# Constant products in three waits of TensorE, four banks more for one chunk, and part of the last norm moved ahead

## The chip, the cores and the metric

The kernel runs as one program on one core of a Trainium2 chip. Its engines are TensorE (PE, with its weight loads as PEld), VectorE (DVE), ScalarE (ACT), GpSimd (POOL) and SyncE (SP), whose queue issues nearly all transfers. The metric is the device time of one execution in microseconds, taken as the median of several executions. Before the change it is 1439.19 us, from three runs between 1438.46 and 1440.05 us.

## The reference

A trunk of two layers over 256 tokens of 1024 features, all in float32. What the change touches is the end of each layer, the first experts of layer 1, and the end of the whole:

```python
for i in range(DEPTH):                                   # DEPTH = 2
    u = rms_norm(h, attn_norm_g[i]) @ w_in[i]            # then three mixers: convolution, SSD, attention
    h = h + concatenate([y_conv, y_ssd, y_mla]) @ w_out[i]
    hn = rms_norm(h, ffn_norm_g[i])
    if i % 2 == 0:
        h = h + swiglu(hn, dense_w_gate[j], dense_w_up[j], dense_w_down[j])
    else:
        h = h + moe_top2(hn, moe_router[j], moe_w_gate[j], moe_w_up[j], moe_w_down[j])   # 8 experts, 2 a token
    gate = sigmoid(rms_norm(h, ple_norm_g[i]) @ ple_w_gate[i])
    h = h + (p[i] @ ple_w_proj[i]) * gate
return rms_norm(h, final_norm_g)
```

`swiglu(h)` is `(silu(h @ wg) * (h @ wu)) @ wd` with 3584 hidden columns, and `rms_norm(x, g)` is `x * rsqrt(mean(x*x) + 1e-6) * g`.

## The kernel before, in words

Every engine has an instruction stream of its own, written out by hand; semaphores tie the streams together, and an engine works through its stream in order. All weights pass through one ring in SBUF, which SP fills in the order in which PE uses it. A transfer into a slot waits until PE has read what was in it.

**Products in parts.** Most products are made exact with three passes: a weight unit `w` that has landed is split by ACT into a high part (`w_hi`, line 1477 or 1483) and by DVE into the rest (`ring_lo`, line 1985 or 1991), and `product` (lines 637 to 639) adds high by high, high by low and low by high. So a unit goes transfer, ACT, DVE, PE. Plain float32 products show two records each, two passes.

**Layer 0, the mixers.** At the end of the mixers PE makes the attention output (bank "pv"), waits until DVE has taken it (`pe.wait_ge(*banks.taken(("pv", L)))`), transposes it (`y_transposed(2, 0)`, line 902), makes the variance product of the convolution (line 911) and the other transposes, and then starts the output projection.

**End of layer 0.** `ple(0)` makes the gates of the embedding add in four groups: half 0 and 1 of the columns, tokens t = 0 and 1. For each group ACT takes the sigmoid (line 1926), DVE multiplies and adds into `h` (lines 2325 and 2329). The norm of layer 1 needs the sum of squares of each group (`square`, line 1501). Before, groups 0 and 1 are squared early and groups 2 and 3 after the last sigmoid and a table load (line 1489); then the roots (1520), the reciprocal (1972), a diagonal matrix of the factors (1977), and PE transposes and scales `h` in one step by 32 passes (line 660). The projections of layer 1 follow.

**The experts.** They are worked in pairs: a heavy one (128 rows, products in parts, `heavy_in`) and a light one (64 rows, plain float32, `light_in`, line 1154) beside each other, in groups of four units of one and four of the other. A unit is 128 x 1792 float32 (0.92 MB); an expert has 48: for each of two chunks of hidden columns 8 units of the gate and 8 of the up matrix, then 16 of the down matrix. The ring has 8 slots for them. The first pair starts with the 16 heavy units of its first chunk, none of the light expert beside them. The gate product of a chunk fills banks 0 to 3; ACT takes the silu out of them (line 1787); then the up product fills the same banks 0 to 3, so its first unit waits for the silu (`g_free`); then DVE multiplies both (line 2481, `gated`), and the gate product of the next chunk waits for that (`u_free`). Banks 4 to 7 belong to the light expert and to transposes.

**The end.** After the last expert, `last_x(0)` transposes half of `h` (line 658), ACT and DVE split it (1529 and 2002), and PE makes the gates of layer 1. After the last add into `h` come the last square, the roots, the reciprocal, and four steps of DVE (line 2674), each `xs = h * rstd * gfin` over 128 x 512; after each one SP writes that quarter out (line 1435). `gfin` is the final norm weight, spread over the partitions.

## Time and profile before

| what | value |
|---|---|
| median of 3 runs | 1439.19 us (1438.46 to 1440.05) |
| the profiled execution, its own time | 1440.5 us |
| its span, first to last instruction | 1438.7 us |
| PE busy | 1387.9 us (96%), mean granted clock 0.991 |
| DVE busy | 854.1 us (59%) |
| ACT busy | 695.3 us (48%) |
| moved by DMA | 443.89 MB, mean 309 GB/s |

The profile is of one execution. Busy shares are means over stages that have different limits: layer 0 runs to about 398 us, the front of layer 1 and the routing to about 538, the experts to about 1400, and the rest is the last embedding add and the last norm. PE's granted clock is a share of full speed: 1.00 is 2.4 GHz and 0.50 is 1.2 GHz.

### The profile page before, as it was taken

The page shows a single profiled execution, that of the slowest core. Times are in us where ns is not written, and L with a number is a line of the kernel's source. Part 1 is how long each engine was busy: PE and PEld are TensorE (multiplying, and loading weights), DVE is VectorE, ACT ScalarE, POOL GpSimd, SP SyncE. Part 2 cuts the span into 40 slices and gives each one's busy share as a digit, 9 for nine tenths or more (in the row PEclk, how much of TensorE's full clock was granted, in tenths as well). Part 3 has the DMA queues.
Part 4 walks back from the last instruction along what each step waited for, and adds up shares of the span by engine and source line. Part 5 has one row for each costly group of instructions (what it writes and reads, how often), then busy time and mean ns, then how long its engine had stood idle before and what let it go on. Part 6 is the DMA issues. An engine that isn't in the chain of part 4 may idle for free.

```text
span 1438.7 us, 18295 instructions
## 1 busy us (share of the span) xinstructions
PE 1387.9 (96%) x6999; PEld 1007.7 (70%) x6999; DVE 854.1 (59%) x986; ACT 695.3 (48%) x783; POOL 6.9 (0%) x14
## 2 busy tenths in 40 slices
PE   6999999999989998999999999999999999999996
PEld 6878888888887787766666666666666666666535
DVE  6997645463479978646454656454656455565425
ACT  6556534542555657544444444444444454544315
POOL 0000000000000000000000000000000000000000
PEclk9999999999999999999999999999999999999998
DMA  9425565555544009999999999999999999999992
GB/s 326 159 69 172 177 199 180 177 200 181 176 136 146 8 8 418 363 421 419 419 405 418 419 419 420 414 404 419 418 420 418 416 412 419 418 419 419 419 410 80
DMA packets 99669, 443.89 MB, mean 309 GB/s; under 512 B 7728, under 2 KB 22096, under 8 KB 99328
## 3 DMA queue, kind: packets, MB, share of 16 engines
q1 hardware_dynamic: 98688, 439.30, 78.1%
q0 software_dynamic: 896, 3.44, 0.7%
q8 instruction: 56, 0.92, 0.3%
q14 instruction: 29, 0.24, 0.0%
HBM read 440.61 MB, written 2.10 MB: 308 GB/s over the span
## 4 chain that ended last, share of the span: by engine, by line
PE 83%; DMA 7%; DVE 6%; ACT 2%; issue 1%; DVEq 0%; ACTq 0%; SPq 0%
PE psum L637 19%; PE psum L638 18%; PE psum L639 18%; PE psum L1154 11%; PE psum L1168 7%; DMA ring<-in_moe_w_up 4%; DMA ring<-in_moe_w_down 3%; PE psum L682 2%; PE psum L1066 1%; PE psum L700 1%; PE psum L660 1%; ACT w_hi L1483 1%; DVE arena_a L2078 1%; PE psum L1183 1%; DVE ring_lo L1991 1%
## 5 line engine op out<-in xcount | busy, mean ns | idle before, releaser
L1991 DVE TENSOR_TENSOR ring_lo<-ring,w_hi 128x1792 fp32r<-128x1792 f32 x191 | 384.3, 2023 | 281.1 <-ACT w_hi L1483 279.0
L1483 ACT ACTIVATE w_hi<-ring 128x1792 fp32r<-128x1792 f32 x191 | 323.3, 1700 | 289.2 <-DMA ring<-in_moe_w_down 121.1
L639 PE MATMUL psum<-w_hi,hidden_b 128*128 128x512 f32 x624 | 230.1, 369 | 0.0
L1985 DVE TENSOR_TENSOR ring_lo<-ring,w_hi 128x2048 fp32r<-128x2048 f32 (+1 forms) x68 | 152.6, 2266 | 102.5 <-ACT w_hi L1477 102.4
L1154 PE MATMUL psum<-ring,xT 128*64 128x512 f32 (+1 forms) x1024 | 201.7, 543 | 0.0
L637 PE MATMUL psum<-w_hi,hidden_b 128*128 128x512 f32 (+1 forms) x512 | 191.3, 374 | 5.2 <-ACT arena_b L1787 3.4
L638 PE MATMUL psum<-ring_lo,hidden_b 128*128 128x512 f32 (+1 forms) x512 | 187.7, 367 | 0.0
L637 PE MATMUL psum<-w_hi,xT_parts 128*128 128x512 f32 (+1 forms) x384 | 150.4, 392 | 4.0 <-DVE xT_parts L2002 3.4
L637 PE MATMUL psum<-w_hi,hidden_a 128*128 128x512 f32 (+1 forms) x384 | 146.7, 382 | 3.6 <-DVE ring_lo L1991 3.6
L1154 PEld LDWEIGHTS psum<-ring,xT 128*64 128x64 f32 x1024 | 69.8, 137 | 114.1 <-issue 112.0
L639 PE MATMUL psum<-w_hi,xT_parts 128*128 128x512 f32 (+1 forms) x384 | 149.2, 389 | 0.0
L638 PE MATMUL psum<-ring_lo,xT_parts 128*128 128x512 f32 (+1 forms) x384 | 149.1, 388 | 0.0
L638 PE MATMUL psum<-ring_lo,hidden_a 128*128 128x512 f32 (+1 forms) x384 | 143.1, 373 | 0.0
L1477 ACT ACTIVATE w_hi<-ring 128x2048 fp32r<-128x2048 f32 (+1 forms) x68 | 126.3, 1898 | 29.2 <-PE psum L639 27.8
L639 PEld LDWEIGHTS psum<-w_hi,hidden_b 128*128 128x128 f32 x624 | 117.6, 188 | 20.8
L637 PEld LDWEIGHTS psum<-w_hi,hidden_b 128*128 128x128 f32 x512 | 96.8, 189 | 34.0 <-issue 9.5
L1168 PE MATMUL psum<-ring,xT 128*64 128x512 f32 (+1 forms) x512 | 112.8, 545 | 0.6 <-DMA ring<-in_moe_w_down 0.6
L638 PEld LDWEIGHTS psum<-ring_lo,hidden_b 128*128 128x128 f32 x512 | 96.9, 189 | 16.0
L639 PE MATMUL psum<-w_hi,hidden_a 128*128 128x512 f32 (+1 forms) x272 | 99.3, 365 | 0.0
L637 PEld LDWEIGHTS psum<-w_hi,hidden_a 128*128 128x128 f32 x384 | 72.3, 188 | 21.3 <-DVE ring_lo L1991 9.3
L637 PEld LDWEIGHTS psum<-w_hi,xT_parts 128*128 128x128 f32 x384 | 72.7, 189 | 18.4 <-DVE ring_lo L1996 3.6
L639 PEld LDWEIGHTS psum<-w_hi,xT_parts 128*128 128x128 f32 x384 | 72.5, 189 | 14.2
(333 smaller groups left out, 1448.3 us busy)
## 6 DMA issues: line engine op xcount, KB each, us to landing
ring<-in_moe_w_gate SPq DMA_DIRECT2D x128, 896.0 KB, 8.9
ring<-in_moe_w_up SPq DMA_DIRECT2D x128, 896.0 KB, 9.9
ring<-in_moe_w_down SPq DMA_DIRECT2D x128, 896.0 KB, 9.8
ring<-in_w_in SPq DMA_DIRECT2D x16, 1024.0 KB, 5.7
ring<-in_dense_w_gate SPq DMA_DIRECT2D x14, 1024.0 KB, 5.1
ring<-in_dense_w_up SPq DMA_DIRECT2D x14, 1024.0 KB, 5.1
ring<-in_dense_w_down SPq DMA_DIRECT2D x14, 1024.0 KB, 4.9
ring<-in_w_out SPq DMA_DIRECT2D x8, 1024.0 KB, 5.0
```

The source lines that it names most:

```text
L637: mm(o, a[0], b[0], start=first, stop=False)
L638: mm(o, a[0], b[1], start=False, stop=False)
L639: return mm(o, a[1], b[0], start=False, stop=final)
L660: last = mm(o[:, c:c + P], h[:, t, kt * P:kt * P + P], diag[:, t, :], start=True, stop=True)
L682: last = mm(o[:, m * SEQ:m * SEQ + SEQ], w[:, kt, m * P:m * P + P], xT[kt], start=kt == 0, stop=kt == KT - 1)
L700: last = mm(o[:, 0:n], xT[kt][:, t * P:t * P + P], w[:, q, :], start=kt == 0, stop=kt == KT - 1)
L1154: last = mm(psum[half * LIGHT:half * LIGHT + LIGHT, 4 + b, 0:n], xl[:, kt, :], w[:, a:a + n], start=kt == 0, stop=kt == KT - 1)
L1168: last = mm(psum[half * LIGHT:half * LIGHT + LIGHT, 2 if tail else 6, c0:c0 + n], elT(kt), w[:, a:a + n], start=kt == 0, stop=kt == FKT - 1)
L1477: A(high(g, sizes[g]), raw(g, sizes[g]), ACT.Copy).then_inc(hi_ready, 1)
L1483: A(heavy_high(c), moe_raw(m), ACT.Copy).then_inc(hi_ready, 1)
L1985: V.tensor_tensor(low(g, sizes[g]), raw(g, sizes[g]), f32(high(g, sizes[g])), ALU.subtract).then_inc(lo_ready, 1)
L1991: V.tensor_tensor(moe_low(m), moe_raw(m), f32(heavy_high(c)), ALU.subtract).then_inc(lo_ready, 1)
```

## The change

A new helper `keep_running(n, b)` makes `n` plain float32 products of constants (the identity by 512 columns of the parameters) into bank `b`, whose content nobody needs. It is called in three places: once with one product ahead of the wait for "pv" in layer 0, once with four after `ple(0)`, once with three after `last_x(0)`.

The first pair's first up chunk goes to banks 4 to 7 (`up_bank`), so that it doesn't wait for the silu, and the next gate chunk waits for the silu instead of for `gated`. The light expert's first gate chunk and the transposes of the heavy hidden part wait for `gated` of that chunk.

In layer 0 the square of group 2 moves ahead of the last sigmoid (it stood there in layer 1 already). In layer 1 DVE multiplies each group of `h` by the final norm weight as soon as it is added (`gained`), and the last step is then one factor a token: DVE does it for t = 0, ACT for t = 1, and SP writes the quarters by halves instead of by tokens.

```diff
+            def keep_running(n, b):
+
+                pe.wait_ge(banks.free[b], banks.count[b])
+                for _ in range(n):
+                    mm(psum[:, b, :], ident, par[:, 0:512], start=True, stop=True)
...
+                if L == 0:
+                    keep_running(1, 3)
                 pe.wait_ge(*banks.taken(("pv", L)))
                 y_transposed(2, 0)
...
                 if L == 0:
                     dense()
                     ple(0)
+                    keep_running(4, 4)
...
             last_x(0)
+            keep_running(3, 3)
...
+        def up_bank(i, ch):
+
+            return 4 if isinstance(i, int) and i == 0 and ch == 0 else 0
...
+                b0 = up_bank(i, ch) if u else 0
+                if b0 and kt == 0:
+                    pe.wait_ge(lx_ready, 1)
                 for b in range(4):
                     if kt == 0 and b < 2:
                         if u:
-                            pe.wait_ge(g_free, half_done(i, ch, b))
+                            if not b0:
+                                pe.wait_ge(g_free, half_done(i, ch, b))
+                        elif ch and up_bank(i, ch - 1):
+                            pe.wait_ge(g_free, half_done(i, ch - 1, b))
                         elif ch:
                             pe.wait_ge(u_free, half_done(i, ch - 1, b))
...
-                    last = product(psum[:, b, 0:cols.stop - cols.start], at((xg_hi, xg_lo), ALLP, kt), at(w, ALLP, cols),
+                    last = product(psum[:, b0 + b, 0:cols.stop - cols.start], at((xg_hi, xg_lo), ALLP, kt), at(w, ALLP, cols),
...
                 elif kt == 0 and ch:
                     pe.wait_ge(lu_free, ch_done(i, ch - 1))
+                elif kt == 0 and up_bank(i, 0):
+                    pe.wait_ge(u_free, half_done(i, 0, 1))
...
-                pe.wait_ge(u_free, half_done(i, ch, (t0 + n - 1) // RUN))
+                pe.wait_ge(u_free, half_done(i, ch, 1 if up_bank(i, ch) else (t0 + n - 1) // RUN))
...
-                    flat = psum[:, 0:4, :].rearrange("p b c -> p (b c)")
+                    flat = psum[:, up_bank(i, ch):up_bank(i, ch) + 4, :].rearrange("p b c -> p (b c)")
...
-            for t in range(NT):
-                for half in range(2):
-                    sp.wait_ge(out_ready, 2 * t + half + 1)
-                    c = slice(half * 512, half * 512 + 512)
+            for half in range(2):
+                c = slice(half * 512, half * 512 + 512)
+                for t, there in enumerate((out_ready, out_scaled)):
+                    sp.wait_ge(there, half + 1)
                     sp.dma_start(out[0, t * P:t * P + P, c], xs[:, t, c]).then_inc(out_done, 16)
...
-                    norm(3 * L, h_added, squared=2)
+                    norm(3 * L, h_added, squared=3)
...
-                        if L == DEPTH - 1 and half and t:
-                            square(3 * DEPTH, 2, h_added)
+                        if half and t:
+                            square(3 * L + 3, 2, h_added)
...
             norm(3 * DEPTH, h_added, squared=3)
+            act.wait_ge(last_rstd, 1)
+            act.wait_ge(gained, 4)
+            for half, buf in enumerate((sg, hs)):
+                A(xs[:, 1, half * 512:half * 512 + 512], buf[:, 1, :], ACT.Copy, scale=rstd[:, 1:2]).then_inc(out_scaled, 1)
...
                         V.tensor_tensor(v, v, buf[:, t, :], ALU.add).then_inc(h_ready, 1)
+                        if L:
+                            if half == t == 0:
+                                dve.wait_ge(gfin_in, 16)
+                            dve.wait_ge(h_ready, 4 * L + 2 * half + t + 1)
+                            V.tensor_tensor(buf[:, t, :], v, gfin[:, cols], ALU.mult).then_inc(gained, 1)
...
             means_of(k, by_half=True)
-            rstd_of(k)
-            dve.wait_ge(gfin_in, 16)
-            for t in range(NT):
-                for c in (slice(0, 512), slice(512, D)):
-                    V.scalar_tensor_tensor(out=xs[:, t, c], in0=h[:, t, c], scalar=rstd[:, t:t + 1], in1=gfin[:, c],
-                                           op0=ALU.mult, op1=ALU.mult).then_inc(out_ready, 1)
+            dve.wait_ge(rms_ready, NT * (k + 1))
+            V.reciprocal(rstd, rms).then_inc(last_rstd, 1)
+            dve.wait_ge(last_rstd, 1)
+            dve.wait_ge(gained, 4)
+            for half, buf in enumerate((sg, hs)):
+                V.tensor_scalar(xs[:, 0, half * 512:half * 512 + 512], buf[:, 0, :], rstd[:, 0:1], None,
+                                ALU.mult).then_inc(out_ready, 1)
```

## Rows read from the trace of the kernel before

**Rows 1.** The page, part 2: GB/s in 40 slices of 36 us.

```profile
GB/s 326 159 69 172 177 199 180 177 200 181 176 136 146 8 8 418 363 421 419 419 405 418 419 419 420 414 404 419 418 420 418 416 412 419 418 419 419 419 410 80
```

**Rows 2.** Waits of PE: who waited for whom, us in total, times, longest.

```profile
PE psum L660 <- DVE xs L1977: 15.8, 2, 11.1
```

**Rows 3.** Windows: busy time by engine, PE's granted clock, DMA share, GB/s.

```profile
402.00:404.00 2.00, 0.97 (x4) 0.98 (x5) 1.68 (x4) 2.00 (x3) 0.00 (x0) 0.50 0.41 140
...
1402.00:1404.00 2.00, 0.00 (x0) 0.00 (x0) 2.00 (x2) 2.00 (x3) 0.00 (x0) 0.50 1.07 414
```

**Rows 4.** Timeline, plain float32 products: start us, us, what, count, idle before.

```profile
99.36 1.12 PE L873 MATMUL psum<-arena_a,par 128*128 128x512 f32 x2
...
537.60 3.81 PE L1056 MATMUL psum<-small,xs 128*128 128x128 f32 x32 [0.86 <-DVE small L2424]
```

**Rows 5.** Timeline of PE and DVE around the "pv" wait of layer 0.

```profile
104.65 0.89 PE L902 MATMUL psum<-par,xs 128*128 128x128 f32 x4 [1.54 <-DVE xs L2249]
...
108.66 0.75 DVE L2001 TENSOR_TENSOR xT_parts<-psum,xT_parts 128x256 fp32r<-128x256 f32 x2
...
109.51 0.47 PE L637 MATMUL psum<-w_hi,xT_parts 128*128 128x512 f32 x1 [0.51 <-issue]
```

**Rows 6.** Timeline of ACT, DVE and PE from layer 0 to layer 1.

```profile
399.76 0.69 DVE L2329 TENSOR_TENSOR h<-h,arena_b 128x512 f32<-128x512 f32 x1
...
400.43 0.61 ACT L1501 ACTIVATE xs<-h 128x512 f32<-128x512 f32 x1
...
403.03 6.54 PE L660 MATMUL psum<-xs,h 128*128 128x128 f32 x32 [4.75 <-DVE xs L1977]
...
409.29 0.19 PEld L637 LDWEIGHTS psum<-xT_parts,w_hi 128*128 128x128 f32 x1
```

**Rows 7.** Timeline of the first pair: PE at both waits, DVE's and ACT's splits.

```profile
569.21 0.77 PE L637 MATMUL psum<-w_hi,hidden_b 128*128 128x512 f32 x1 [3.43 <-ACT arena_b L1787]
...
571.49 3.96 DVE L1991 TENSOR_TENSOR ring_lo<-ring,w_hi 128x1792 fp32r<-128x1792 f32 x2 [2.60 <-ACT w_hi L1483]
...
587.25 1.71 ACT L1483 ACTIVATE w_hi<-ring 128x1792 fp32r<-128x1792 f32 x1 [0.42 <-DMA ring<-in_moe_w_gate]
...
591.66 0.47 PE L637 MATMUL psum<-w_hi,hidden_b 128*128 128x512 f32 x1 [1.27 <-DVE arena_b L2481]
...
608.15 1.70 ACT L1483 ACTIVATE w_hi<-ring 128x1792 fp32r<-128x1792 f32 x1 [1.29 <-DMA ring<-in_moe_w_gate]
```

**Rows 8.** Windows of 10 us after the first chunk, columns as in rows 3.

```profile
580.00:590.00 10.00, 10.00 (x52) 8.47 (x51) 8.11 (x5) 6.96 (x5) 0.00 (x0) 1.00 0.97 379
590.00:600.00 10.00, 8.73 (x47) 7.09 (x46) 4.71 (x4) 0.60 (x1) 0.00 (x0) 1.00 0.96 348
600.00:610.00 10.00, 10.00 (x52) 5.33 (x51) 6.89 (x5) 7.29 (x5) 0.00 (x0) 1.00 0.98 331
```

**Rows 9.** Timeline of PE after the last expert, to its last instruction.

```profile
1404.86 0.77 PE L637 MATMUL psum<-w_hi,xT_parts 128*128 128x512 f32 x1 [3.41 <-DVE xT_parts L2002]
...
1409.54 1.03 PE L658 MATMUL psum<-par,h 128*128 128x128 f32 x8
1410.33 0.48 PE L637 MATMUL psum<-w_hi,xT_parts 128*128 128x512 f32 x1
...
1429.24 0.39 PE L639 MATMUL psum<-w_hi,xT_parts 128*128 128x512 f32 x1
```

**Rows 10.** Timeline of the last norm and of the writes.

```profile
1433.37 2.74 DVE L2674 SCALAR_TENSOR_TENSOR xs<-h,tiny,arena_a 128x512 f32<-128x512 f32 x4
...
1434.15 2.32 SPq L1435 DMA_DIRECT2D out<-xs  x4
```

**Rows 11.** Window at the writes' end, columns as in rows 3.

```profile
1436.00:1438.00 2.00, 0.00 (x0) 0.00 (x0) 0.11 (x1) 0.00 (x0) 0.00 (x0) 0.50 0.90 335
```

**Rows 12.** Two windows that have PE waits, columns as in rows 3.

```profile
850.00:860.00 10.00, 8.21 (x43) 4.73 (x42) 7.73 (x6) 6.80 (x4) 0.00 (x0) 1.00 1.01 419
...
1400.00:1402.00 2.00, 1.19 (x8) 0.76 (x8) 2.00 (x4) 0.94 (x3) 0.00 (x0) 1.00 1.07 392
```

More of the change, by code:

```diff
@@ L366, in trunk @@
             "ptok_in", "last_ptok_in", "gfin_in", "out_ready", "out_done"))
+        out_scaled, last_rstd, gained = sem("out_scaled"), sem("last_rstd"), sem("gained")
         table_in, eps_ready = sem("table_in"), sem("eps_ready")
@@ L2327, in embed @@
                             dve.wait_ge(*banks.taken(("pp", L, half, t)))
-                        v = h[:, t, half * 512:half * 512 + 512]
+                        cols = slice(half * 512, half * 512 + 512)
+                        v = h[:, t, cols]
                         V.tensor_tensor(v, v, buf[:, t, :], ALU.add).then_inc(h_ready, 1)
+                        if L:
[3 more added lines that the diff above has]
+                            V.tensor_tensor(buf[:, t, :], v, gfin[:, cols], ALU.mult).then_inc(gained, 1)
                     if L == 0 and half == 0:
```

## The prediction

> **What bounds the kernel now.** I read the page first. From 540 us to about 1400 us it shows 404 to 421 GB/s in every slice but one, the one from 575 to 611 us, which has 363 [rows 1]. So the experts are bound by their transfers. Only in that slice do the transfers fall short, and time saved on PE among the experts counts only where PE holds back a transfer. All else runs at far lower rates and is bound by PE or by chains between PE, ACT and DVE.
>
> Then the waits of PE. The longest is for the diagonal matrices ahead of the transposes of a layer, 15.8 us in two, of which 11.1 us is the start of the kernel, which nothing here touches; the other is 4.7 us [rows 2]. Then the granted clock in windows: behind that wait PE works at 0.50, and so it does behind the last expert [rows 3]. The timelines show what each wait is for and what is late next.
>
> **Three waits with constant products.** The price of a product: one of 128x512 in plain float32 takes 1.12 us alone, in two passes [rows 4]. That is the upper end for each in a row; for the lower, 32 passes of 128 columns take 3.81 us, 0.12 each [rows 4]. Passes overlap, so I take 0.9 a product, an estimate from below 1.12.
>
> *Layer 0, "pv".* PE idles 1.54 us before 104.65 [rows 5], so one product fits (1.12 at most). What PE does next at the half clock could be faster, but the first product of the output projection starts at 109.51, right after DVE's part of the transposes ends (108.66 + 0.75 = 109.41 [rows 5]), and DVE comes there from the norm factors and a split of weights, not from PE. From there PE has work without a pause. So nothing is gained: 0, with 0 to 1 us for executions in which the clock falls a little later and is still low after 109.51.
>
> *Into layer 1.* Four products behind the last gate (PE idle from 403.03 - 4.75 = 398.28 [rows 6]) end between 398.28 + 4 x 0.9 = 401.9 and 398.28 + 4 x 1.12 = 402.8. The wait now ends at 403.03, and by the next edit at 402.57, so at worst they cost 0.2. Before, PE did nothing from 398.28, its clock was at 0.50 by 402 [rows 3], and the 32 transposing passes took 6.54 us [rows 6]. The same number of passes of the same 128 columns at the full clock took 3.81 [rows 4]. Gain: 6.54 - 3.81 = 2.7. What is late next: ACT and DVE split each of four banks, 0.85 us each on both, beside PE; the first projection needs the banks one after the other, and its first weight load came at 409.29, behind the transposes [rows 6], so I let it follow them.
>
> *The square moved ahead.* ACT's squares start at 400.43 and take 0.61 each [rows 6]; one of the two goes to a place where ACT idles, ahead of the last sigmoid. The remaining one can't start before DVE's add is done, 399.76 + 0.69 = 400.45, later by 0.09 because the sigmoid now waits for the moved square: 400.54 and a handover of 0.04, against a start of 401.04 (400.43 + 0.61). Gain 0.46, let me call it 0.5. Together 3.2 us into layer 1. That part is a chain of PE, then DVE, and its transfers are far from full (146, 8 and 8 GB/s [rows 1]), so I pass all 3.2 on to the start of the experts' loads.
>
> *After the last expert.* PE idles 3.41 us before 1404.86 [rows 9], waiting for DVE; three products end between 1401.45 + 2.7 = 1404.2 and + 3.36 = 1404.8, inside it. Behind it PE works at 0.50: the 12 products up to the transposes at 1409.54 take 4.68 us. At the full clock 84 products run from 1410.33 to 1429.24 [rows 9], 0.228 each, and 12 take 2.73. Gain 1.95. The weights and the second half of the transposed rows then have to come 1.95 earlier; they hang on PE's own transposes, and the splits of the later units have over 1 us to spare, so I take 1.9.
>
> **The first up chunk in banks of its own.** PE stands 3.43 us before 569.21 for the silu and 1.27 us before 591.66 for DVE's product of the chunk [rows 7]; both waits go, and the clock doesn't drop behind the first. PE could go on at 565.8. A unit takes it 9 x 0.228 + 3 x 0.114 = 2.4 us, so the fourth is due at 573.0; its low part comes from DVE, which starts it at 571.49 with 3.96 us for two [rows 7], so it is there at 573.5: 0.5 us lost. Another 0.5 goes to the first transposes of the hidden part, which now wait for all of DVE's product. PE still gains about 5 us. But the loads gain only what they had lost for want of free slots: from 580 to 610 us they moved 379, 348 and 331 GB/s [rows 8] against 420, which is (41 + 72 + 89) x 10 / 420 = 4.8 us. The landings show less: two splits of ACT that waited for their load start at 587.25 and 608.15 [rows 7], eight loads of 0.92 MB apart, 20.9 us where 420 GB/s give 17.5: 3.4 lost. I take the middle, 4.1, and keep 3.4 to 4.8. From 610 us on the loads run full in either kernel, so all later events move by the same 4.1. The lights' new wait and the chunk's wait for the silu are over long before they are reached.
>
> **The last norm.** Before, four steps of DVE take 2.74 us from 1433.37 [rows 10]; after, two short ones on DVE and two of 0.62 on ACT (its square has the same width [rows 6]), so the last quarter is ready about 1.3 us sooner. The added four products with the weight, 0.69 each, lie in DVE's waits for the gates, except the last: it stands before DVE's share of the mean, which ACT's root needs, and costs 0.1. The wait for the weight's transfer moves ahead with them; POOL issues it right behind the last expert, long before DVE reaches the first of the four, and I cost it at nothing. But the writes are 1.05 MB. DVE made a quarter of 262 kB every 0.685 us, 383 GB/s, and in the last window the DMA engines are busy 0.90 of the 2 us [rows 11], though the writes end near 1437.8: they were already saturated. So the end follows the first issue, 1434.15 [rows 10], not the last. The first quarter's step reads one operand from memory where the old one read two; no row has it at this width, it lies between 0 and 0.69, and I take 0.45. The first issue then comes 0.69 - 0.45 - 0.1 sooner. Gain 0.2, from -0.1 to 1.3 if the writes do speed up.
>
> **Sum.** 0 + 3.2 + 4.1 + 1.9 + 0.2 = 9.4 us. The profiled execution took 1440.5 (span 1438.7 and 1.8 around it), which gives 1431.1; the median of the runs is 1.3 lower, 1439.19, and from it I get 1429.8.
>
> **The rivals.**
>
> *The last fall of the clock comes anyway.* Ahead of it, in 1400 to 1402 us, PE was busy for 1.19 of 2.00 us, nearly all of it transposes, and the clock fell at the end. In 850 to 860 us, PE stood still for 1.79 us among ordinary products and the clock stayed at 1.00 [rows 12]. So the transposes may not have held it, and three products behind them may come too late; part of them would then run at half speed and PE would start some 0.7 late, with the clock back sooner than before. From 1.9 to about 0.6: 1431.1. The Trainium skill, page "TensorE: Matmul & The Clock Gate", section "Part 4: PE-mode transpose", says that transposes in that mode don't count as PE work for the clock in the way that products do; by that rule this rival would be the likelier one. The trace agrees as far as those two windows go.
>
> *The loads keep their pace.* If the loss from 580 to 610 us came from the order of loads of heavy and light units and not from PE, the 4.1 are gone: 1433.9. Against it: each load waits for a slot that PE frees, and they are short right after PE's two waits.
>
> *The products don't hold the clock at all.* Then 0.5 is left of the 3.2, and three products at half speed, up to 6.7 - 1.12 = 5.6 us, delay PE by some 2 us from 1404.86 in place of helping; with the clock back at 1408.8 as before this costs 0.8. 0.5 + 4.1 - 0.8 + 0.2 = 4.0: 1435.2.
>
> *Slower.* PE comes to the second pair with more lead than the loads (5 against 4.1), so it waits there for longer. If the clock fell in such waits, as it did in the 3.43 us of the first pair, each fall would cost PE 1.6 us (8 products at 0.43 in place of 0.228), and loads behind it. About eight waits like that of 850 to 860 [rows 12] are spread over the pairs. From the sixth fall on the gain is gone; all eight give 1429.8 + 12.8 = 1442.6. Against it: that wait of 1.79 us left the clock at 1.00, and the lead is used up after one pair.
>
> **How the numbers follow.** My forecast 0.62, the last clock fall 0.16, loads keep their pace 0.09, products don't hold 0.07, slower 0.03, and 0.03 for two of the failures together (about 1438). The range 1427.5 to 1434.3: below the forecast lie 0.7 of the loads (4.8), up to 1 in layer 0 and up to 1.1 in the writes, not all at once; above it the next two rivals. A measurement of this kernel tells about 0.2%, 2.9 us. Faster than 1436.3 are the first four cases nearly always: 0.92. Within 0.2%: 0.05. Slower: 0.03.
>
> **What would show it.** In the new profile: the clock at 1.00 through 400 to 412 us and the transposes in about 3.8 us; no wait of PE for the silu, and over 400 GB/s in each window from 580 to 610 us; the clock at 1.00 behind the last expert, the 12 products in 2.7 us; the writes still at about 380 GB/s from first to last. The prediction is wrong if the experts' part is as long as before, if a later window falls below 400 GB/s by as much as the first pair won, or if PE is late behind its products.

## The result and the profile after

The changed kernel takes 1428.67 us (median of 4 runs, 1428.14 to 1431.9) against 1438.83 before (4 runs, 1438.36 to 1440.05): a ratio of 0.993, 95% interval 0.9916 to 0.9944, so 10.2 us less. The forecast was 1429.8 and the range 1427.5 to 1434.3.

The profiled executions stand further apart, 1428.27 against 1440.5. Four marks that both traces have divide their 12.2 us: the landing of the first of the experts' loads, of the 40th (PE's two waits in the first pair lie before it), of the last, and the end of PE.

```
                                   before    after   less
start to first landing             541.98   537.82   4.16
first to 40th landing               94.11    88.92   5.19
40th to last landing               758.88   757.29   1.59
last landing to PE's end            34.65    33.48   1.17
PE's end to the end                  9.04     8.95   0.09
```

Not all of it is sure to belong to the change. PE is 0.96 us ahead at the output projection of layer 0, and it was so already at 25 us, where nothing was edited. Nothing was edited between the 40th and the last landing either. That stretch takes 757.0 to 757.8 us in nine profiles of kernels with the four banks and 757.5 to 759.4 in five without them, so the two sets overlap and one pair can't tell. Without these two, 4.16 - 0.96 + 5.19 + 1.17 + 0.09 = 9.65 us are left.

The three places of the constant products, in the changed kernel. First the timeline of PE at "pv", against [rows 5] (start us, us, what, count, idle before):

```profile
101.99 1.08 PE L674 MATMUL psum<-par 128*128 128x512 f32 x2
...
103.68 0.66 PE L913 MATMUL psum<-par,xs 128*128 128x128 f32 x4 [0.62 <-DVE xs L2276]
...
108.55 0.47 PE L642 MATMUL psum<-w_hi,xT_parts 128*128 128x512 f32 x1 [1.78 <-DVE ring_lo L2012]
```

One product is two passes, 1.08 us. What follows it is quicker, but the first product of the output projection now waits 1.78 us for DVE and starts 0.96 us sooner than before, the same 0.96 that PE was ahead from 25 us on.

Then DVE, ACT and PE into layer 1, against [rows 6]:

```profile
396.84 0.63 ACT L1524 ACTIVATE xs<-h 128x512 f32<-128x512 f32 x1 [1.48 <-DVE h L2357]
...
397.18 3.59 PE L674 MATMUL psum<-par 128*128 128x512 f32 x8
...
398.89 0.69 DVE L2357 TENSOR_TENSOR h<-h,arena_b 128x512 f32<-128x512 f32 x1
...
399.62 0.63 ACT L1524 ACTIVATE xs<-h 128x512 f32<-128x512 f32 x1
...
401.62 3.84 PE L665 MATMUL psum<-xs,h 128*128 128x128 f32 x32 [0.85 <-DVE xs L2004]
...
405.19 0.19 PEld L642 LDWEIGHTS psum<-xT_parts,w_hi 128*128 128x128 f32 x1
```

The second square stands alone behind DVE's last add, the other is at 396.84, ahead of the sigmoid. The four products take 3.59 us, the transposes 3.84 in place of 6.54, and the first projection starts 4.10 us sooner than before: 3.1 more than the 0.96 that were there already.

Then PE after the last expert, against [rows 9], and the windows there and into layer 1, against [rows 3] (busy time by engine, PE's granted clock, DMA share, GB/s):

```profile
1389.53 1.45 PE L663 MATMUL psum<-par,h 128*128 128x128 f32 x7 [0.27 <-DVE h L2535]
1390.78 4.00 PE L674 MATMUL psum<-par 128*128 128x512 f32 x6
1394.22 0.79 PE L642 MATMUL psum<-w_hi,xT_parts 128*128 128x512 f32 x1
...
1397.39 1.03 PE L663 MATMUL psum<-par,h 128*128 128x128 f32 x8
```

```profile
402.00:404.00 2.00, 2.00 (x21) 2.00 (x20) 2.00 (x2) 1.78 (x4) 0.00 (x0) 1.00 0.00 1
...
1390.00:1392.00 2.00, 2.00 (x7) 1.46 (x6) 2.00 (x3) 1.82 (x5) 0.00 (x0) 0.50 1.07 397
...
1394.00:1396.00 2.00, 2.00 (x8) 1.32 (x7) 2.00 (x3) 0.00 (x0) 0.55 (x1) 1.00 0.67 277
```

Into layer 1 the clock stays at 1.00. After the last expert it falls all the same, during the transposes and before the products, which therefore take 4.00 us; but it is back when the 12 products begin, and they take 3.17 us in place of 4.68.

The first pair, in windows of 10 us against [rows 8]. No window is short of transfers any more:

```profile
570.00:580.00 10.00, 10.00 (x51) 8.45 (x50) 9.11 (x5) 6.97 (x5) 0.00 (x0) 1.00 1.01 424
580.00:590.00 10.00, 10.00 (x55) 8.44 (x54) 8.72 (x7) 4.29 (x4) 0.00 (x0) 1.00 1.01 419
590.00:600.00 10.00, 10.00 (x51) 5.29 (x50) 4.74 (x3) 5.61 (x4) 0.00 (x0) 1.00 1.01 418
600.00:610.00 10.00, 10.00 (x54) 8.07 (x54) 5.17 (x4) 3.50 (x5) 0.00 (x0) 1.00 1.02 421
```

Last, the norm and the writes, against [rows 10]:

```profile
1421.43 1.33 ACT L1969 ACTIVATE xs<-arena_b,tiny 128x512 f32<-128x512 f32 x2 [0.23 <-DVE tiny L2704]
1421.43 0.88 DVE L2708 TENSOR_SCALAR xs<-arena_b,tiny 128x512 f32<-128x512 f32 x2
1421.95 1.82 SPq L1458 DMA_DIRECT2D out<-xs  x4
```

The four writes are issued within 1.82 us in place of 2.32. They land at 1423.99, 1424.70, 1425.37 and 1426.05; before at 1436.22, 1436.90, 1437.58 and 1438.26. Both are 0.67 to 0.71 us apart, and the last lands 4.10 and 4.11 us after the first issue. The 0.5 us that the last issue gained is gone before it lands.

### The profile page after: what moved, and what is told of

It reads as the page before. It is cut to its first block, busy times and chain, and to the rows that moved or that the text cites. A ratio compares the mean times of both kernels' runs of the same rounds, so it can differ in the third digit from the quotient of the medians.

```text
span 1426.5 us, 18333 instructions
## 1 busy us (share of the span) xinstructions
PE 1387.9 (97%) x7015; PEld 1004.9 (70%) x7015; DVE 854.5 (60%) x988; ACT 697.4 (49%) x785; POOL 6.9 (0%) x14
## 4 chain that ended last, share of the span: by engine, by line
PE 84%; DMA 6%; DVE 6%; ACT 2%; issue 1%; ACTq 0%; DVEq 0%; SPq 0%
PE psum L642 19%; PE psum L643 18%; PE psum L644 18%; PE psum L1176 11%; PE psum L1190 7%; DMA ring<-in_moe_w_up 4%; DMA ring<-in_moe_w_down 2%; PE psum L693 2%; PE psum L1080 1%; PE psum L711 1%; ACT w_hi L1506 1%; PE psum L1205 1%; DVE arena_a L2105 1%; DVE ring_lo L2018 1%; PE psum L665 1%
```

## The experiments

The theory to be tested: the loads of the first pair carry half of the gain, and they gain what they were short of, not what PE gains; the clock carries nearly all of the rest, in two places; "pv" and the last norm carry nothing. The first four kernels put one part each into the kernel before.

**The four banks alone.**

```diff
+        def up_bank(i, ch):
+            return 4 if isinstance(i, int) and i == 0 and ch == 0 else 0
...
-                    last = product(psum[:, b, 0:cols.stop - cols.start], ...
+                    last = product(psum[:, b0 + b, 0:cols.stop - cols.start], ...
```

> The kernel before with the four banks for the first pair's first up chunk and nothing else. Theory 'transfers' (the gain is what the loads lost for want of free slots): the slices from 580 to 610 us move over 410 GB/s, the loads of the first pair's end come 4.0 us sooner, and the time falls by 4.0 to 4.8 us although PE gains 5 us or more in that pair. Rival 'PE': all that PE gains is passed on, 5.5 to 6 us. Rival 'the load that came late': of the 5.2 us that the changed kernel gained there, 1.2 us was one load that came late in the one profiled execution of the kernel before; then the medians differ by 4.0 and no more.

Measured: 1433.69 us (6 runs, 1431.84 to 1434.63) against 1439.01 (29 runs, 1435.94 to 1444.11, which the four kernels share): a ratio of 0.9964 (0.9952 to 0.9977), 5.3 us less. The 40th load lands 89.6 us after the first, against 94.1 before. The windows from 580 us:

```profile
580.00:590.00 10.00, 10.00 (x51) 8.46 (x50) 9.28 (x6) 6.80 (x4) 0.00 (x0) 1.00 1.01 422
590.00:600.00 10.00, 10.00 (x55) 7.50 (x56) 4.24 (x5) 3.25 (x4) 0.00 (x0) 1.00 1.03 419
600.00:610.00 10.00, 10.00 (x53) 6.45 (x50) 7.29 (x4) 5.16 (x4) 0.00 (x0) 1.00 1.00 391
```

Two windows are full, the third lacks 29 x 10 / 420 = 0.7 us. So this part is the largest. Its 5.3 lies above the 4.1 of the forecast, but the interval of the ratio, 3.3 to 6.9 us, has room for all three: the theory (4.0 to 4.8), "PE" (5.5 to 6) and "the load that came late" (4.0). The load that came late in the kernel before (the 39th, by 1.2 us) was no accident of one execution: in each of the four other profiles of kernels without the banks, that load or the one before it loses another 0.5 to 0.9.

**The four products into layer 1 alone.**

```diff
                     dense()
                     ple(0)
+                    keep_running(4, 4)
```

> The kernel before with the four constant products into layer 1 and nothing else; the square stays where it was. Theory 'clock': the 32 passes that transpose take 3.8 us in place of 6.5, everything after comes 2.7 us sooner up to the experts' first loads and stays so to the end: 2.7 us less. Rival 'the loads take it back': the experts' loads begin no sooner or wait for something else, and less than 1 us is left at the end.

Measured: 1435.98 us (12 runs, 1434.48 to 1439.93), ratio 0.9984 (0.9975 to 0.9994): 3.0 us less by the medians, 2.3 (0.9 to 3.6) by the ratio. The products and the transposes take as long as in the changed kernel:

```profile
397.55 3.60 PE L669 MATMUL psum<-par 128*128 128x512 f32 x8
...
402.46 3.84 PE L660 MATMUL psum<-xs,h 128*128 128x128 f32 x32 [1.31 <-DVE xs L1984]
```

Its profile shows something else at the first pair. The wait for the silu is the same as in [rows 7], but the clock didn't fall behind it: the first window is this kernel's, the second the kernel before's.

```profile
565.57 0.47 PE L637 MATMUL psum<-w_hi,hidden_b 128*128 128x512 f32 x1 [3.41 <-ACT arena_b L1794]
```

```profile
568.00:572.00 4.00, 4.00 (x22) 3.37 (x21) 4.00 (x3) 3.00 (x2) 0.00 (x0) 1.00 1.02 425
```

```profile
568.00:572.00 4.00, 2.79 (x7) 2.24 (x8) 1.40 (x2) 3.99 (x5) 0.00 (x0) 0.64 1.01 399
```

**The three products after the last expert alone.**

```diff
             last_x(0)
+            keep_running(3, 3)
```

> The kernel before with the three constant products after the last expert and nothing else. Theory 'the clock falls before the products and is back after them' (as in the changed kernel's trace): the products run at half speed, some 4 us for the three, and end about when PE's wait ends; the 12 products behind them run at the full clock, 3.2 us in place of 4.7, and 1.6 us is gained. If the clock falls later in this kernel, by the place of its end, the products themselves or the first of the 12 run slow and 0.6 us is left. Rival 'the products only delay': no gain, or up to 0.8 us lost.

Measured: 1437.04 us (11 runs, 1434.76 to 1439.72), ratio 0.9988 (0.9976 to 0.9999): 2.0 us less by the medians, 1.7 (0.1 to 3.5) by the ratio. PE:

```profile
1398.44 1.75 PE L658 MATMUL psum<-par,h 128*128 128x128 f32 x7 [0.27 <-DVE h L2509]
1399.99 3.53 PE L669 MATMUL psum<-par 128*128 128x512 f32 x6
1402.95 0.79 PE L637 MATMUL psum<-w_hi,xT_parts 128*128 128x512 f32 x1
...
1406.12 1.04 PE L658 MATMUL psum<-par,h 128*128 128x128 f32 x8
```

The clock falls before the products here too and is back at their end; the 12 products take 3.17 us. From the last landing to the first product behind the second transposes it is 14.05 us, against 15.36 before: 1.3 gained in these two executions.

**The last norm alone.**

```diff
-            for t in range(NT):
-                for half in range(2):
-                    sp.wait_ge(out_ready, 2 * t + half + 1)
...
+                for t, there in enumerate((out_ready, out_scaled)):
+                    sp.wait_ge(there, half + 1)
...
+                            V.tensor_tensor(buf[:, t, :], v, gfin[:, cols], ALU.mult).then_inc(gained, 1)
```

> The kernel before with the changed last norm and nothing else (the products with the weight ahead, the second half of the last step on ACT, the writes in the other order). Theory 'writes bind': the first write is issued 0 to 0.2 us sooner and the last lands as long after it as before (4.1 us): 0 to 0.2 us gained. Rival 'the last quarter binds': the last write is issued 0.5 us sooner after the first, so it lands 0.5 us sooner or more: 0.5 to 1.3 us gained.

Measured: 1439.15 us (11 runs, 1435.17 to 1440.54), ratio 1.0003 (0.9994 to 1.0012): nothing. The last write lands 4.10 us after the first issue, and the interval excludes the rival's 1.3 us, though not its 0.5; the landings exclude that.

By the medians the four parts give 5.3 + 3.0 + 2.0 - 0.1 = 10.2 us, the whole 10.2. That they agree to a tenth is luck: by the ratios they are 5.2 + 2.3 + 1.7 - 0.4 = 8.8, each known to some 1.3 to 1.8 us, and the square is in none of them.

**The writes on two queues**, in the changed kernel, to see what binds them.

```diff
-                    sp.dma_start(out[0, t * P:t * P + P, c], xs[:, t, c]).then_inc(out_done, 16)
+                sp.dma_start(out[0, 0:P, c], xs[:, 0, c]).then_inc(out_done, 16)
...
+                act.dma_start(out[0, P:2 * P, c], xs[:, 1, c]).then_inc(out_done, 16)
```

> The changed kernel with the two writes of the second 128 rows issued by ACT, right behind its own scaling, in place of SP. Theory 'the writes bind, at the rate of the memory or the DMA engines': they land 0.68 us apart as before, and the end stays within 0.1 us of 4.1 us after the first issue. Rival 'one queue binds': the two queues' writes land side by side, and the end comes 0.5 us sooner.

Measured: 1429.36 us (5 runs, 1427.94 to 1429.5), ratio 0.9929 (0.9916 to 0.9943). The issues:

```profile
1423.09 0.83 SPq L1457 DMA_DIRECT2D out<-xs  x2
1423.33 0.95 ACTq L1972 DMA_DIRECT2D out<-xs  x2
```

They land at 1425.14, 1425.88, 1426.53 and 1427.18, the last 4.09 us after the first issue, though the last is issued 0.85 us behind the first in place of 1.37. Two queues move no more than one. While the writes are under way the DMA engines are full in both kernels; the first window is the changed kernel's, the second this one's:

```profile
1424.00:1425.00 1.00, 0.00 (x0) 0.00 (x0) 0.00 (x0) 0.00 (x0) 0.00 (x0) 0.50 1.01 375
```

```profile
1424.00:1425.00 1.00, 0.00 (x0) 0.00 (x0) 0.00 (x0) 0.00 (x0) 0.00 (x0) 0.50 1.01 383
```

So the writes bind there (262 kB in 0.68 us, 385 GB/s), and what the last norm gains behind its first issue is lost before the end. The median is 1.2 us above that of the unchanged kernel in the same series (1428.16), so the second queue gained nothing either. Writes of another size were not tried.

**Three products in front of the first up chunk**, in the changed kernel: how much of PE's gain the loads needed.

```diff
                 if b0 and kt == 0:
                     pe.wait_ge(lx_ready, 1)
+                    for _ in range(3):
+                        mm(psum[:, b0, :], ident, par[:, 0:512], start=True, stop=True)
```

> The changed kernel with three constant products put ahead of the first pair's first up chunk, where PE no longer waits: PE is held up there by some 2.8 us at the full clock. Theory 'the loads have a little slack': PE gained about 1 us more in that pair than the loads took, and 0.5 us of it was a wait for DVE's split that the products now cover; so 1.3 to 1.8 us are lost, and they are missing in the slices from 580 to 610 us. Rival 'PE is not what holds the loads': nothing is lost. Rival 'PE holds them at every step': all 2.8 us are lost.

Measured: 1431.68 us (6 runs), ratio 0.9942 (0.9928 to 0.9956). That is 3.0 and 3.5 us above the two medians of the changed kernel (1428.67, and 1428.16 in the run after the next): more than the theory's 1.3 to 1.8, and nearest to the rival "PE holds them at every step" with its 2.8. But the six lie in two groups: 1429.2, 1429.7, 1430.3, and 1433.1, 1433.3, 1433.8. The profile is of the second:

```profile
540.00:550.00 10.00, 10.00 (x44) 8.77 (x44) 8.29 (x7) 7.92 (x7) 0.00 (x0) 0.66 1.02 425
...
590.00:600.00 10.00, 10.00 (x55) 7.27 (x55) 4.39 (x5) 4.60 (x4) 0.00 (x0) 1.00 1.00 370
600.00:610.00 10.00, 10.00 (x53) 6.69 (x50) 6.18 (x4) 4.00 (x3) 0.00 (x0) 1.00 0.98 375
```

Here the clock was low from 541 to 548 us as well, which makes PE later still. The first group lost 0.5 to 2.1 us, which is the theory's size, but these three have no profile, and that no fall came there in them isn't shown. So the theory is neither shown nor out; "nothing is lost" is out by the medians.

**Three products in the wait for the silu**, in the kernel before: what of the gain was the clock.

```diff
+                if u and kt == 0 and ch == 0 and isinstance(i, int) and i == 0:
+                    pe.wait_ge(lx_ready, 1)
+                    for _ in range(3):
+                        mm(psum[:, 4, :], ident, par[:, 0:512], start=True, stop=True)
```

> The kernel before with three constant products in PE's wait for the silu of the first pair (into bank 4): the wait stays, the clock doesn't fall behind it. Theory 'two parts' (the executions in which the clock happened not to fall there missed 3.1 and 3.8 us of loads from 580 to 610 us, those in which it fell 4.8): 1.0 to 1.8 us gained, and the rest needs the wait to go. Rival 'it was the wait alone': 0. Rival 'it was the clock alone': 4 us or more.

Measured: 1438.67 us (11 runs, 1437.46 to 1439.51) against 1439.63 (17 runs), ratio 0.9995 (0.9986 to 1.0004): 1.0 us less by the medians, at most 2.0 by the ratio, and it may be nothing. "The clock alone" is out. The profile can't tell the other two apart: the clock fell at 544 us in it, PE came late to the wait, and the products then held it up. ACT has the first half of the silu at 568.6, PE goes on at 569.67. That is 28.7 us after the first landing, where the last norm alone, whose clock fell in the same place, has 27.6.

```profile
567.69 1.73 ACT L1791 ACTIVATE arena_b<-psum 128x896 f32<-128x896 f32 x2 [0.82 <-PE psum L639]
...
567.50 2.73 PE L1108 MATMUL psum<-par 128*128 128x512 f32 x6
569.67 0.80 PE L637 MATMUL psum<-w_hi,hidden_b 128*128 128x512 f32 x1
```

**The changed kernel once more.**

> The changed kernel unchanged, for the spread of its own executions beside those with single edits: 1428.5 us, with some executions 1.5 to 3.5 us longer. Theory 'falls of the clock at the experts' first products make the long ones': a profile of a short one shows the clock at 1.00 from 530 to 600 us.

Measured: 1428.16 us (5 runs, 1427.91 to 1428.42). No execution was long, and the profiled one of 1427.91 had the low clock from 540 to 547 us:

```profile
540.00:550.00 10.00, 10.00 (x42) 8.74 (x42) 8.29 (x7) 8.06 (x7) 0.00 (x0) 0.66 1.01 422
```

So a fall there doesn't by itself make an execution of this kernel long; what made the one of 1431.9 is open. With this run the loads can be set beside PE's lateness. Against the changed kernel's first profile: how much later SP could issue the 31st load, counted from the first issue, and how much later the 40th landed, counted from the first landing.

```
                                    issue  landing   the clock fell
changed, once more                   1.89     0.11   at 540
four banks alone                     1.90     0.71   at 544
products into layer 1 alone          4.38     3.25   not there
changed, three products in front     4.45     4.18   at 541
last norm alone                      5.05     3.57   at 543
before                               6.08     5.19   at 569, behind the silu
before, products in the silu's wait  6.25     4.71   at 544
```

1.9 us of lateness cost the loads 0.1 to 0.7 (three more profiles of kernels with the banks, those with two queues and with DVE in another order, have the same 1.9 and lose 0.4). With 4.4 to 6.3 us of it they land 3.3 to 5.2 later. So there is some slack, and it is why a fall of the clock costs little in the changed kernel; no run lies between 1.9 and 4.4, so where the slack ends isn't shown.

**Without the product of "pv".**

```diff
-                if L == 0:
-                    keep_running(1, 3)
```

> The changed kernel without the constant product of layer 0. Theory: the first product of the output projection waits for DVE in either case, and nothing is lost, 0 within 0.3 us, with the clock low or not in the stretch from 103 to 110 us. Rival: the product carries the clock past the start of the output projection, and 0.5 to 1 us is lost without it.

Measured: 1428.8 us (5 runs, 1428.52 to 1430.38), ratio 0.9927 (0.9914 to 0.994), as the changed kernel. The clock was at 0.50 from 105.4 to 108.8 us, and yet:

```profile
106.00:108.00 2.00, 2.00 (x4) 0.86 (x5) 2.00 (x4) 0.38 (x2) 0.00 (x0) 0.50 0.00 0
...
104.66 0.66 PE L913 MATMUL psum<-par,xs 128*128 128x128 f32 x4 [1.53 <-DVE xs L2274]
...
109.53 0.47 PE L642 MATMUL psum<-w_hi,xT_parts 128*128 128x512 f32 x1 [0.30 <-issue]
```

From the end of the "pv" wait to the output projection 4.87 us pass with the product missing and the same 4.87 with it (103.68 to 108.55), because DVE sets the second time. The product could go.

**Two half products ahead of the last transposes.**

```diff
+            keep_running(1, 3, 256)
             pe.wait_ge(lyh_ready, n_iter)
...
+            keep_running(1, 3, 256)
             last_x(0)
             keep_running(3, 3)
```

> The changed kernel with two more constant products of half the width after the last expert, one in PE's wait for the hidden part of the lights (0.69 us) and one in its wait for the add before the last transposes (0.81 us). Theory 'the clock falls for what PE did before the transposes': it stays at 1.00 past 1391 us more often, the eight transposes take 1.0 us in place of 1.45, what hangs on them comes 0.3 to 0.5 us sooner, and 0.3 to 0.5 us is gained. Rival 'too little': the clock falls in the same place and the time stays. Rival 'they delay': the halves don't fit into their waits, and 0.2 to 0.4 us is lost.

Measured: 1428.76 us (5 runs, 1427.85 to 1430.29): no change. The clock stayed at 1.00, but it did so in two profiles without the halves too (the kernel without the product of "pv", and the changed kernel once more), so this says nothing of the halves. What it does say stands in the once-more profile:

```profile
1390.65 2.74 PE L674 MATMUL psum<-par 128*128 128x512 f32 x6
1394.23 0.47 PE L642 MATMUL psum<-w_hi,xT_parts 128*128 128x512 f32 x1 [0.83 <-DVE xT_parts L2029]
```

At the full clock the products are done 0.8 us too soon: DVE sets this stretch. It adds four quarters to h, of which the first transposes need two, then splits weights, then makes the low parts that PE waits for.

**DVE in another order there.**

```diff
-                for n in (0, 2, 1, 3):
+                for n in (0, 2):
                     add_back(n_iter - 1, 1, n, LAST_SCATTER[n])
                 after_split(n_iter, 0)
+                late[:] = [lambda n=n: add_back(n_iter - 1, 1, n, LAST_SCATTER[n]) for n in (1, 3)]
...
                         take_xT(3 * L + 2, L, "g_ple", (2 * half, 2 * half + 1))
+                        while late:
+                            late.pop(0)()
                         after_split(n_iter, 1 + half)
...
-            keep_running(3, 3)
+            keep_running(2, 3)
```

> The changed kernel with DVE's work after the last expert in another order: the two adds that only the last four transposes need come behind the split of the first weights and the low parts of the first transposes, and two constant products stand there in place of three. Theory 'DVE sets this stretch': PE starts the 12 products 1.4 us sooner after the last load (two adds of 0.68 us), and the next 12 at DVE's second split, some 1.2 us sooner; 0.7 to 1.3 us gained. Rival 'given back at the next wait': the adds now delay the second split or the squares of ACT, and the end moves by less than 0.3 us.

Measured: 1427.11 us (5 runs, 1426.5 to 1429.91), 1.05 below the changed kernel in the same series (1428.16, 1427.91 to 1428.42). The two sets of runs overlap, so this run alone doesn't show a gain. In the profile the clock fell in the first transposes, and PE was held by its own products:

```profile
1390.45 1.76 PE L663 MATMUL psum<-par,h 128*128 128x128 f32 x7 [0.27 <-DVE h L2535]
1391.99 2.81 PE L674 MATMUL psum<-par 128*128 128x512 f32 x4
1394.24 0.79 PE L642 MATMUL psum<-w_hi,xT_parts 128*128 128x512 f32 x1
```

**The same with one product.**

```diff
-            keep_running(2, 3)
+            keep_running(1, 3)
```

> The changed kernel with the two late adds moved behind, as in the kernel with another order, and one constant product after the last expert in place of its two. In that kernel's profile the clock was low from the first transposes on and the two products took 2.8 us, so that they, and not DVE, held PE till 9.3 us after the last load. Theory 'PE waits for its own products': with one, PE starts the 12 products 8.2 to 8.8 us after the last load whether the clock is low or not; if it is low, the first of the 12 run slow and 0.5 us of it goes back; up to 0.5 us less than with two, 1426.6 to 1427.1 us. Rival 'one doesn't hold the clock': the clock falls behind it in executions in which it would have stayed, and 0.5 to 1.5 us is lost.

Measured: 1426.92 us (4 runs, 1426.54 to 1427.43) against 1440.19 (7 runs), ratio 0.9912 (0.9896 to 0.9929), the lowest median of all kernels here; the slowest of the four is below the fastest of the nine runs of the changed kernel (1427.91).

```profile
1389.79 0.98 PE L663 MATMUL psum<-par,h 128*128 128x128 f32 x7 [0.27 <-DVE h L2535]
1390.61 1.02 PE L674 MATMUL psum<-par 128*128 128x512 f32 x2
1392.87 0.47 PE L642 MATMUL psum<-w_hi,xT_parts 128*128 128x512 f32 x1 [1.23 <-DVE xT_parts L2029]
```

PE starts the 12 products 8.6 us after the last landing, against 10.2 (clock low) and 9.9 (clock at 1.00) in the changed kernel, and ends 31.5 us after it, against 33.5 and 32.8. At the full clock in both, that is 1.3 us less. DVE and not the products ended PE's wait in the changed kernel (0.83 us after the last product) and does so here (1.23 us after it), so it is DVE's order that gains. One product was enough in this execution; a low clock didn't occur in it, so whether one is better than two there isn't shown.

## Why the prediction was right, and where its terms were off

The two profiles of the result are one execution each, and executions differ. All fourteen profiles of this document, grouped by whether the kernel has the part that matters in a stretch, give steadier terms (us, mean and spread; the square goes with the products into layer 1).

```
                             without                 with                 less  forecast
start to first landing   541.3 (540.3 to 542.0)  538.2 (537.8 to 538.7)    3.1     3.2
first to 40th landing     93.2 (92.2 to 94.1)     89.1 (88.7 to 89.6)      4.1     4.1
first to last landing    851.6 (850.0 to 853.0)  846.5 (845.9 to 847.1)    5.1     4.1
last landing to PE's end  34.7 (34.2 to 35.6)     33.2 (32.8 to 33.5)      1.5     1.9
PE's end to the end       9.03 (9.01 to 9.04)     8.95 (8.93 to 8.96)      0.1     0.2
```

There are five profiles without the part in each row, and eight, eight, eight, seven and nine with it. Left out are the products without the square in the first row, three products in front in the second and third, and DVE's other order in the fourth.

**"pv", 0.** Right, for the reason given: DVE ends last there. The run without the product shows it, 4.87 us either way.

**Into layer 1, 3.2.** Right: 3.1 in the pair of profiles and over all of them. The products alone, forecast at 2.7, gave 3.0 by the medians, 2.3 by the ratio and 2.5 by the first landing (538.8). The square's 0.5 was not timed by itself; in the profile ACT's last square starts 0.04 us after DVE's add has ended, and PE's wait ends 0.44 us sooner, beyond the 0.96 that PE was ahead.

**The first pair, 4.1.** The mechanism was right. In the five profiles without the banks, the bytes that the windows from 580 to 610 us lack against 420 GB/s come to 4.8, 4.8, 4.4, 3.7 and 3.1 us, and the 40th load lands 5.2, 4.9, 4.7, 3.6 and 3.3 us later after the first than in the changed kernel's first profile. So missing bytes price this stretch up to there. The 3.4 from two splits of ACT was too low for the execution that it was read from, which lost 5.2, because the 39th load lost another 1.2 behind them. That the middle, 4.1, is the mean over all profiles is luck. The step that failed is the one after it: from 610 us on the loads would run full in either kernel, and all later events move by the same 4.1. By the last landing the difference has grown to 5.1, and the banks alone took 5.3 less by the medians (3.3 to 6.9 by the ratio). Most of the further 1.0 is there by the 97th load (4.9); what those loads wait for was not traced.

How much of the loss is the clock's isn't shown. Of the kernels without the banks, the two whose clock fell behind the silu lost 5.2 and 4.9, and the one whose clock stayed up there after the same wait, the products into layer 1 alone, lost 3.3. But the last norm alone, with 3.6, had a fall before the wait and came to it so late that it waited for 1.10 us only, and the kernel with products in the wait gained at most 2.0 us and perhaps nothing.

**After the last expert, 1.9.** The 1.9 holds for an execution whose clock stays up: 1.85 in the second profile of the changed kernel (13.51 us from the last landing to the product behind the second transposes, against 15.36). In the first profile the rival "the last fall of the clock comes anyway" came true: 14.15, a gain of 1.2, not the rival's 0.6, because PE started 0.3 late (10.2 us after the last landing against 9.9) and not 0.7, and the clock was back when the 12 products began. In nine profiles of kernels with constant products there, five show the fall and four don't. The Trainium skill, page "TensorE: Matmul & The Clock Gate", section "Part 4: PE-mode transpose", says that such transposes don't count for the clock as products do; these nine neither confirm nor refute it, since the same transposes stand ahead of both outcomes. What the products do there is plain from where the falls lie. All five come while the first eight transposes run, before the first product. The five profiles without products there all show a fall: one during the transposes (the banks alone), four in the wait behind them. With products, none of the four that are still up falls in that wait. So the products hold the clock where it is still up when they begin, and can't help where it has fallen already.

**The last norm, 0.2.** It is 0.1 by the profiles and nothing by the medians. The prediction's own terms for the first issue give 0.69 - 0.45 - 0.1 = 0.14, which it rounded up to 0.2. The writes bind, as the step said.

**The sum.** 9.4 was forecast, 10.2 came (8.1 to 12.1 by the ratio's interval), and the terms over all profiles add up to 3.1 + 5.1 + 1.5 + 0.1 = 9.8. The experts' loads gained more than forecast, the wait after the last expert less. The other rivals fell: the loads didn't keep their pace, the products do hold the clock into layer 1, and the later windows stayed at 410 GB/s or more to the last full slice of the page:

```profile
GB/s 334 158 66 172 178 191 190 180 182 201 167 150 146 8 5 417 421 419 419 420 413 420 419 418 420 414 416 419 418 419 419 415 415 419 418 420 419 419 410 92
```

## What to carry to other kernels

A stretch that is short of transfers loses what its missing bytes say: this sum over windows came within 0.4 us of the landings in five profiles, the lateness of two single loads did not, and neither told what was lost behind the windows. PE could be 1.9 us late there for 0.1 to 0.7 us of the loads; of 4.4 us, most reached them. Work put into a wait to hold the clock must fit into it at the low clock as well, or it becomes the wait, and before it is added one should ask which engine ends the wait: at "pv" and after the last expert that was DVE, and reordering DVE after the last expert gained another microsecond or so on top of what keeping PE busy had gained. Before single terms are read from two profiles, look which parts of their difference lie where nothing was changed, and put the profiles of all kernels that share a part beside each other.

## What the runs showed of the hardware

The clock's falls aren't bound to a place in the program: behind the same wait of 3.4 us for the silu it went to 0.50 in two profiles and stayed at 1.00 in a third, and at the experts' first products (540 to 551 us), which no edit touched, it stayed up in six profiles of fourteen (both kernels' first ones among them) and was low in eight. Behind the transposes after the last expert it fell in four of the five profiles in which PE then stood idle (in the fifth it had fallen already), and in none of the four in which it was still up when constant products began there. A plain float32 product of constants, 128x512, took 1.02 to 1.08 us alone and 0.90 in a row of four (3.59 us); two in a row took 2.81 us with the clock at 0.50 for the first 1.9. Writes from one queue and from two land 0.65 to 0.74 us apart for 262 kB each, with the DMA engines full.
